# Four of twelve conditioning chunks moved from the first stage into the next one's projections

## The reference

```python
def adaln(cond, w, b):
    mod = (jax.nn.silu(cond) @ w + b).reshape(cond.shape[0], 6, D_MODEL)
    return tuple(mod[:, i][:, None, :] for i in range(6))

sh1, sc1, g1, sh2, sc2, g2 = adaln(c_ctx[None, :], ada_w[l], ada_b[l])
h = rmsnorm(xp, norm1[l]) * (1.0 + sc1) + sh1
out, k_c, v_c, s_f, s_b = token_mixer(h, w_in[l], ...)
xp = xp + g1 * out
h = rmsnorm(xp, norm2[l]) * (1.0 + sc2) + sh2
xp = xp + g2 * conv_ffn(h, w_up[l], conv_w[l], conv_b[l], w_down[l])
```

## Time and profile before

| | us |
|---|---|
| median of 3 runs | 2784.21 |
| lowest and highest | 2783.48, 2798.66 |
| the profiled execution's own time | 2790.27 |
| its span | 2788.5 |
| TensorE, weight loads | 2653.8, 2430.7 busy |
| VectorE, ScalarE, GpSimd | 1664.8, 1026.6, 808.1 busy |

### The profile page before, as it was taken

One profiled execution on the slowest core, in us unless ns is written; L12 is line 12 of the kernel. 1 busy time (PEld: TensorE's weight loads), 2 busy tenths in 40 slices (PEclk: granted clock), 3 DMA queues, 4 the chain that ended last, 5 costly groups with the idle time before them and its releaser, 6 DMA issues. The chain is left out here.

```text
span 2788.5 us, 41208 instructions
## 1 busy us (share of the span) xinstructions
PE 2653.8 (95%) x15025; PEld 2430.7 (87%) x15025; DVE 1664.8 (60%) x2673; ACT 1026.6 (37%) x1899; POOL 808.1 (29%) x775
## 2 busy tenths in 40 slices
PE   5899999999999799999999989799999999999998
PEld 2799999999999787768878867599999999999997
DVE  3245355355455447776777666635677766677765
ACT  3223233223223126666666656533221222221214
POOL 0222122122122143252253231743323232323232
PEclk8999999999999799999999989899999999999999
DMA  9311111111111110020020010331111111111101
GB/s 372 118 38 44 34 39 42 34 40 40 34 41 32 45 34 8 1 60 2 7 68 8 1 51 1 99 98 31 53 45 38 45 38 45 38 45 38 45 23 75
DMA packets 164251, 135.99 MB, mean 49 GB/s; under 512 B 18460, under 2 KB 141884, under 8 KB 164156
## 3 DMA queue, kind: packets, MB, share of 16 engines
q1 hardware_dynamic: 162940, 130.02, 14.8%
q10 hardware_dynamic: 1216, 4.72, 0.4%
HBM read 120.44 MB, written 14.29 MB: 48 GB/s over the span
## 5 line engine op out<-in xcount | busy, mean ns | idle before, releaser
L335 PE MATMUL proj_ps<-act_hi,w_hi 128*128 128x384 f32 x1152 | 410.9, 357 | 6.5 <-POOLq L473 6.5
L335 PE MATMUL ffn_ps<-act_hi,w_hi 128*128 128x384 f32 (+2 forms) x1128 | 385.1, 341 | 12.9 <-PEq L976 8.1
L336 PE MATMUL proj_ps<-act_lo,w_hi 128*128 128x384 f32 x1152 | 390.7, 339 | 0.0
L337 PE MATMUL proj_ps<-act_hi,w_lo 128*128 128x384 f32 x1152 | 390.5, 339 | 0.0
L336 PE MATMUL ffn_ps<-act_lo,w_hi 128*128 128x384 f32 (+2 forms) x1128 | 383.9, 340 | 0.0
L337 PE MATMUL ffn_ps<-act_hi,w_lo 128*128 128x384 f32 (+2 forms) x1128 | 383.9, 340 | 0.0
L2394 DVE SCALAR_TENSOR_TENSOR resid_t<-ffn_ps,mod,resid_t 128x384 f32<-128x384 f32 (+2 forms) x640 | 273.9, 508 | 140.8 <-PE ffn_ps L337 140.8
L1747 DVE TENSOR_TENSOR probs_lo<-att_ps,probs_hi 128x512 fp32r<-128x512 f32 x324 | 223.1, 689 | 157.0 <-ACT att_ps L1544 153.2
L1543 ACT ACTIVATE probs_hi<-att_ps 128x512 fp32r<-128x512 f32 x324 | 193.9, 599 | 199.0 <-PE att_ps L1363 198.1
L2372 DVE SCALAR_TENSOR_TENSOR conv<-up,conv_t,conv 128x127 f32<-128x127 f32 (+1 forms) x168 | 211.9, 1320 | 77.8 <-ACT conv L2300 66.0
L483 POOL CAST w_hi<-w_raw 128x1024 fp32r<-128x1024 f32 x48 | 61.8, 1287 | 628.4 <-PE proj_ps L337 593.5
(11 more groups left out here) (286 smaller groups left out, 5860.5 us busy)
## 6 DMA issues: line engine op xcount, KB each, us to landing
w_raw<-in_w_in SPq DMA_DIRECT2D x64, 512.0 KB, 3.9
ada_w<-in_ada_w SPq DMA_DIRECT2D x12, 2048.0 KB, 14.2
w_raw<-in_w_up SPq DMA_DIRECT2D x44, 512.0 KB, 3.9
w_raw<-in_w_down SPq DMA_DIRECT2D x22, 512.0 KB, 3.6
rec_scratch<-rec_out SPq DMA_DIRECT2D x8, 576.0 KB, 2.8
out<-xy SPq DMA_DIRECT2D x9, 512.0 KB, 2.6
w_raw<-in_w_o SPq DMA_DIRECT2D x8, 512.0 KB, 5.0
xy<-in_x_sample SPq DMA_DIRECT2D x8, 512.0 KB, 5.8
```

Of the source, the lines that this page charges most:

```text
L335: nc.tensor.matmul(out, w_hi, x_hi, start=(k == 0), stop=False)
L336: nc.tensor.matmul(out, w_hi, x_lo, start=False, stop=False)
L337: return nc.tensor.matmul(out, w_lo, x_hi, start=False, stop=last)
```

## The change

Phase 0 handles only eight chunks, in the order 0, 2, 1, 3, 4, 5, 6, 7. The first two give the shift and scale of x's first four column blocks, and the next two those of the other four, so x's parts 0 to 11 need only two chunks. `X_FOR` is a new table: parts 0 to 3 ahead of the third chunk's columns, 4 and 5 ahead of the fourth's, then five parts each ahead of the fifth to seventh and three ahead of the eighth. The first two blocks of `w_in` are issued behind the fourth chunk, the third again at the end. Of each column block's three parts ScalarE now scales the third (`scaled_part`) as well as rounding all three, and `HF` has three buffers.

Chunks 8 to 11 (sc2 and g2) go into phase 1. They use one slot, which lies over `k_dec` and `q_dec` (now one tile). SyncE issues them among the loads of `w_in`. TensorE runs chunk i's columns behind unit i of head 0 (i from 0 to 3) and its rows behind the first group of the next unit. The stationary operand there is `C2`, two columns wide, and the PSUM bank is set to zero first. ScalarE copies out between its unit copies. VectorE adds the result to the bias kept in MOD[32:48] and makes A2 inside `gates(0)`.

```diff
-        NCOL = 12
+MOD_NOW, MOD_LATER = (0, 2, 1, 3, 4, 5, 6, 7), (8, 9, 10, 11)
+        NCOL = len(MOD_NOW)
-        HF = sb("h_f32", [P, 2, 512])
+        HF = sb("h_f32", [P, 3, 512])
-        X_FOR = {c: range(3 * (c - EARLY), 3 * (c - EARLY) + 3) for c in range(EARLY, NCOL)}
+        X_FOR = {2: range(0, 4), 3: range(4, 6), 4: range(6, 11), 5: range(11, 16), 6: range(16, 21), 7: range(21, NX)}
 # SyncE, phase 0
-                    sp.dma_start(AW[:, c % AHEAD], ada[c]).then_inc(ada_in[c % AHEAD], 16)
-                    if c == 9:
+                    sp.dma_start(AW[:, c % AHEAD], ada[MOD_NOW[c]]).then_inc(ada_in[c % AHEAD], 16)
+                    if c == 3:
                         for u in range(2):
                             sp.dma_start(WR[:, u], w_in[first_units[u]]).then_inc(w_raw_in[u], 16)
 # ScalarE, phase 0
+                def scaled_part(n):
+                    j, (t0, t1, grp) = n // 3, GR[n % 3]
+                    act.wait_ge(xt_done, n + 1)
+                    act.wait_ge(mod_ok, 3 if j < 4 else 6)
+                    if n >= 3:
+                        act.wait_ge(lo_done, n - 1)
+                    nc.scalar.activation(HF[:, n % 3, 0:(t1 - t0) * P], xps[:, n % 4, 0:(t1 - t0) * P], ACT.Identity,
+                                         scale=A1[:, j, grp:grp + 1], bias=MOD[:, j, grp:grp + 1]).then_inc(hf_done_a, 1)
+                def column_parts(j):
+                    high_part(3 * j)
+                    scaled_part(3 * j + 2)
+                    high_part(3 * j + 1)
+                    high_part(3 * j + 2)
+                parts_done = 0
                 for c in range(NCOL):
+                    while c in X_FOR and 3 * parts_done + 2 <= X_FOR[c][-1] - 3:
+                        column_parts(parts_done)
+                        parts_done += 1
                     act.wait_ge(ada_done, c + 1)
...
+                for j in range(parts_done, KC):
+                    column_parts(j)
 # TensorE, phase 0
+                columns(0)
+                columns(1)
+                rows(0)
+                rows(1)
                 pe.wait_ge(xn_done, NT)
+                for c in range(2, NCOL):
                     for n in X_FOR[c]:
                         x_part(n)
                     columns(c)
+                    if c == 3:
+                        rows(2)
+                    if c == 3 or c > 4:
+                        rows(c if c == 3 else c - 1)
                 rows(NCOL - 1)
 # VectorE, phase 0
+                nc.vector.tensor_copy(MOD[:, 32:48, :], VT[:, 32:48].unsqueeze(2).broadcast_to((P, 16, 2)))
+                nc.vector.tensor_copy(A2[:, :, :], VT[:, 56:64].unsqueeze(2).broadcast_to((P, 8, 2)))
+                nc.vector.tensor_copy(C2[:, :, :], CS[:, :, 0:2])
...
                 for n in range(NX):
+                    if n in (0, 12):
+                        first_modulation(n // 12)
+                    if n % 3 < 2:
+                        dve.wait_ge(xt_done, n + 1)
+                        if n >= 3:
+                            dve.wait_ge(lo_done, n - 1)
+                        nc.vector.tensor_scalar(HF[:, n % 3, 0:(t1 - t0) * P], xps[:, n % 4, 0:(t1 - t0) * P], ...)
                     if n:
                         low_part(n - 1)
...
 # SyncE, phase 1
+                def load_chunk(i):
+                    if i:
+                        sp.wait_ge(ada_done, i)
+                    sp.dma_start(AW, ada[MOD_LATER[i]]).then_inc(ada_in, 16)
+                load(0, 3)
+                load(0, 4)
+                load_chunk(0)
                 first_states(0)
+                load(0, 5)
+                load_chunk(1)
+                load(1, 0)
+                load_chunk(2)
+                load(1, 1)
+                load_chunk(3)
+                load(1, 2)
+                load(1, 3)
 # TensorE, phase 1
+                def chunk_columns(i):
+                    if i == 0:
+                        pe.wait_ge(ada_zero, 1)
+                    pe.wait_ge(ada_in, 16 * (i + 1))
+                    if i >= 2:
+                        pe.wait_ge(ada_out, i - 1)
+                    for k in range(KC):
+                        q = k % 4
+                        m = nc.tensor.matmul(aps[32 * q:32 * q + 2, i % 2, :], C2[:, k, :], AW[:, k, :], start=(k < 4), stop=(k >= 4))
+                    m.then_inc(ada_done, 1)
                 for u in range(NU):
+                    for g in range(NG):
+                        for part in range(3):
+                            unit_part(0, u, g, part)
+                        if g == 0 and 0 < u <= len(MOD_LATER):
+                            chunk_rows(u - 1)
+                    if u < len(MOD_LATER):
+                        chunk_columns(u)
 # ScalarE, phase 1
+                chunk_evacuate(0)
                 act.wait_ge(zero_ok, 3)
                 for d in range(2):
                     for g in range(NG):
                         evacuate(0, U_RFF + d, g, SIG[:, d], ACT.Sigmoid)
+                    chunk_evacuate(1 + d)
 # VectorE, phase 1, in gates(0) behind the wait for the first exponentials
+                    dve.wait_ge(mod_t, len(MOD_LATER))
+                    nc.vector.tensor_tensor(MOD[:, 32:48, :], MOD[:, 32:48, :], kvps[:, 0, 0:32].rearrange(...), ALU.add).then_inc(mod_sum, 1)
+                    dve.wait_ge(mod_sum, 1)
+                    nc.vector.scalar_tensor_tensor(A2[:, :, :], MOD[:, 32:40, :], 1.0, A2[:, :, :], ALU.add, ALU.mult).then_inc(mod_ok, 1)
```

More of the change, by code:

```diff
@@ L110, in build, with phase0 @@
         phase3(nc, a, sem, W, HH, HL, MOD, CW, A2, X1, w_o, w_up, w_down, ident, ones, y_prompt, y_sample)
-def phase0(nc, a, sb_, pb_, sem, W, w_in, first_units, HH, HL, ident, ones, CW, MOD, A1, A2, lb, lb1, lb1n, rgain):
+MOD_NOW, MOD_LATER = (0, 2, 1, 3, 4, 5, 6, 7), (8, 9, 10, 11)
+def phase0(nc, a, sb_, pb_, sem, W, w_in, first_units, HH, HL, ident, ones, CW, MOD, A1, A2, lb, lb1, lb1n, rgain, C2, SEL):
     with ExitStack() as ctx:
@@ L238, in rows @@
                     pe.wait_ge(ada_out, c + 1)
-                    if c >= EARLY:
+                    if c >= 4:
                         pe.wait_ge(vec_ok, 2)
                         pe.wait_ge(lo_done, 1)
-                    out = mps if c < EARLY else vps
-                    for b in range(4 * c, 4 * c + 4):
-                        m = nc.tensor.matmul(out[:, 2 * b:2 * b + 2], MR[:, c % 2, (b - 4 * c) * P:(b - 4 * c + 1) * P], SEL[:, :], start=True, stop=True)
+                    out = mps if c < 4 else vps
+                    b0 = 4 * MOD_NOW[c]
+                    for b in range(b0, b0 + 4):
+                        m = nc.tensor.matmul(out[:, 2 * b:2 * b + 2], MR[:, c % 2, (b - b0) * P:(b - b0 + 1) * P], SEL[:, :], start=True, stop=True)
                     m.then_inc(mod_t, 1)
@@ L346, in load_qkv, with phase1 @@
         sp.dma_start(WR[:, 0, :, HEAD:P], w_in64[kv + 2 * B_V]).then_inc(done, 16)
-def phase1(nc, a, sem, W, w_in64, HH, HL, ident, ones, lb, lb1, lb1n, rgain, w_in, rec_dram, out_state, spent):
+def phase1(nc, a, sem, W, w_in64, HH, HL, ident, ones, lb, lb1, lb1n, rgain, w_in, rec_dram, out_state, spent, MOD, A2, C2, SEL):
     with ExitStack() as ctx:
@@ L585, in sum_squares, with chunk_rows @@
                     nc.tensor.matmul(kvps[:, g % 2, 0:G], ones[:, :], SQ[:, g * G:(g + 1) * G], start=True, stop=True).then_inc(ss_done, 1)
-                for u in range(NU):
-                    unit(0, u)
+                def chunk_columns(i):
[8 more added lines that the diff above has]
+                    m.then_inc(ada_done, 1)
+                def chunk_rows(i):
+                    pe.wait_ge(ada_out, i + 1)
+                    for b in range(4):
+                        n = 4 * i + b
+                        m = nc.tensor.matmul(kvps[:, 0, 2 * n:2 * n + 2], MR[:, i % 2, b * P:(b + 1) * P], SEL[:, :], start=True, stop=True)
+                    m.then_inc(mod_t, 1)
+                for u in range(NU):
+                    for g in range(NG):
[5 more added lines that the diff above has]
+                        chunk_columns(u)
                 pe.wait_ge(zero_ok, 3)
+                pe.wait_ge(mod_ok, 1)
                 with pe.Fori(0, RH - 1) as r:
@@ L752, in gates @@
                         dve.wait_ge(exp_f, h * 2 + (d + 1))
+                        if behind_mod and d == 0:
+                            last_modulation()
                         last = GB[:, d, CH - 1:T:CH] if d == 0 else GB[:, d, 0:T:CH]
@@ L807, in normalise @@
                         nc.vector.tensor_tensor(OT[:, cols], OT[:, cols], RG[:, cols], ALU.mult).then_inc(rec_ready, 1)
-                gates(0)
+                gates(0, True)
                 dve.wait_ge(m_in, 16)
```

86 lines of the change are left out of this document (47 added, 39 removed).

## The result

The changed kernel takes 2757.0 us (median of 8 runs, 2754.8 to 2773.0), against 2784.0 for the kernel before on the same chip: a ratio of 0.9905, 95% interval 0.9884 to 0.9926. It gains 27 us, near 1% of the time. The prediction was 2774.6, a gain of 9.6, with a range down to 2769. The profiled execution took 2771.75 us, span 2769.9; it lies above most runs of its kernel, as the one of before does, so stages are compared by their own rows. Part of the difference is TensorE's granted clock: from 900 to 1200 us it was 0.91 in this execution, 0.94 in the one of before, and 0.96 in a second profile of the changed kernel (h1_after_again, span 2755.3).

What follows compares the result with a forecast made beforehand. The prediction took ada_w transfers plus a tail to bound the kernel up to 96.15 us, and TensorE after. Terms of -21.6 and +12.0 sum to -9.6, so 2774.6 us as median, range 2769 to 2786.

Steps and rivals of the forecast that it cites:

- any gain above 24: Whole kernel: a measured gain of more than 24 us was listed as a sign that the prediction is wrong.
- even with no cost at all in phase 1 the gain is 21.6: Whole kernel: 21.6 us as the most to gain, used to argue that no case reaches a 1% change, 27.8 us.
- the time from the first projection to the end longer by 12: From the first projection on: 12 us longer, listed as a sign that the prediction is right.
- Part 1: Phase 0: four of twelve ada_w transfers go, 21.7 us; the new chunk 7 is there at 64.1 us.
- Part 2: Phase 0, x's parts: start at 34.5 us, VectorE ends at 72.2, stage shorter by 21.6 us, bounds 17.3 and 23.4.
- the columns of chunks 4 to 7 start at 46.3, 54.0, 61.6 and 65.6: Phase 0: start times in us from laying out three engines' operations in the new order, with columns at 2.5 us.
- Rival (A): Phase 0 bound by TensorE's and ScalarE's chain at the lower clock: VectorE ends at 76.5, -17.3 us, total 2778.9; chance 0.14.
- Its tail is no shorter than before: End of phase 0: VectorE's tail stays as long, from ScalarE's last column of x and GpSimd's subtraction for the third w_in block.
- Part 3: Head 0's projections: four added chunks cost 12.0 us of TensorE, from 11.1 to 15.3; the added waits cost nothing.
- (B): Phase 1: chunk columns lose their overlap with two-column weights, 31.8 us for four chunks; total +10.2 us, 2794.4; chance 0.08.
- (C): Phase 1: chunks come late, TensorE stands some 3 us at each of three and its clock drops; +1.4, 2785.6; chance 0.06.
- (D): Phase 0: early w_in blocks leave a queue gap ahead of chunk 4, losing 5.4 of 21.6 us; 2780.0; chance 0.06.

Runs made afterwards that it cites:

- e1: The kernel before with only an unused tile of 96 bytes a partition ahead of w_raw: 2760.1 us, ratio 0.9911.
- g1: The changed kernel, but ScalarE handles a column block of x ahead of a chunk's copy whenever its transposes precede the chunk's columns: 2749.4 us, ratio 0.9872.
- e5: The kernel before with an unused tile of 32 bytes a partition ahead of act_hi, so that everything moves: 2779.4 us, ratio 0.9974.
- e6: The kernel before with an unused tile of 32 bytes a partition between act_hi and act_lo: 2777.3 us, ratio 0.9972.
- e3: The kernel before with an unused tile of 32 bytes a partition ahead of w_raw: 2758.2 us, ratio 0.9902.

## Why the prediction was wrong

The total failed for want of a term: what the moved tiles do to the products. The prediction said of the kept tiles that their copies cost "nothing", and never asked what else their 96 bytes do. They shift every tile behind them, and 22.5 us by the rows, 24.1 by e1, came of that. No rival named it, and the line "any gain above 24" among the signs of an error was the only guard. The bound for "even with no cost at all in phase 1 the gain is 21.6" was a bound on the steps considered, not on the kernel. The same shows in its sign "the time from the first projection to the end longer by 12": it is 2769.9 - 80.31 = 2689.6 us for 2788.5 - 96.15 = 2692.3, shorter by 2.7, and by 17 in h1_after_again (2755.3 - 80.09).

With placement put aside, point by point:

- Part 1, transfers: right. Four chunks are 21.7 us of transfers, and the new chunk 7 lands at 64.1, as g1 shows.
- Part 2, the parts of x: wrong by 6 us. The step that failed is the layout's "the columns of chunks 4 to 7 start at 46.3, 54.0, 61.6 and 65.6". They started 4 to 7 us later and the stage was shorter by 15.8, not 21.6. The layout chose 2.5 us for the columns, where chunks 4 and 6 took 3.58 and 3.39, and had GpSimd's holding some 2 us too late (43 to 50, in fact 41.4 to 48.1). What it had for ScalarE's order cannot be read, since its operations are not on record; g1 shows that this wait, with the clock that went along with it, was worth 8 us: there the projections start at 72.18, sooner than the 74.5 forecast. Rival (A), with chance 0.14 and -17.3 us, named the mechanism and was near its size; g1 shows the chain of engines, by taking it away, and the lower clock was seen but not tried by itself.
- "Its tail is no shorter than before": wrong, in the kernel's favour, and at odds with the layout's own 72.2 - 65.6 = 6.6. VectorE ends 77.90 - 72.50 = 5.4 us after the start of chunk 7's columns, against 93.82 - 85.89 = 7.9 before. The columns came so late that the third w_in block was on hand at 66.08 and split before the tail began, so no subtraction of GpSimd's held act_lo there. It hid part of what the circle cost.
- Part 3, the cost in phase 1: right, 12.0 forecast, 11.7 measured. The overlap with two columns of weights is the one of 32 (1.90 us for 16 instructions), so (B) is out. No wait of TensorE for a transfer after 80 us, so (C) is out. VectorE's cover is 9 us for the 8 forecast. Its sum rests on 1.92 and 1.05 us for columns and rows; they took 1.90 and 0.95.
- (D): out; chunk 7's transfer was in time.

So the staging itself gave -15.8 + 11.7 = -4.1 by the trace and -3.1 by the medians of the changed kernel and e1_pad96, where -9.6 was forecast. The sign of the staging was right and its size was not; the measured 27 us is that and 24 us of placement. The placement was luck: with `C2` and `SEL` behind the weight tiles (e2) the same change gains nothing that can be measured (ratio 1.0009).

The Trainium skill (GPSIMD Engine Reference, Key points) says that VectorE's instructions with two SBUF inputs contend with GpSimd. The trace agrees: the two-input act_lo took 1.89 us beside the subtraction, and 0.69 alone (the one of 55.92). The Trainium skill (TensorEngine Tiling (Array Packing), Key Properties) has a drain at each change of tiling mode. With 1.83 us from the start of the columns to the next product, no more is seen here than what the columns themselves take.

## What to carry to other kernels

A change that adds or removes a kept tile moves all tiles behind it; compare the addresses of the hot operands in both builds before the stages are compared, and test with an unused tile in the kernel before. In this kernel a moving tile and its weights that lie alike modulo 64 bytes save 0.08 us in each group of 24 products of 384 columns, 24 us in all, for 32 or 96 unused bytes in a partition. And when transfers leave a stage that they bounded, lay the engines' hand-written order against each other: here one condition in ScalarE's stream (work that is ready goes ahead of a copy that still waits) was worth 7.6 us, more than the whole move of the chunks.

## What the runs showed of the hardware that was not expected

- The spacing of products with 384 columns at clock 1.00 depends on how the moving operand and the weights lie to each other modulo 64 bytes: 0.173 us where both lie at 0, 0.177 where one lies at 0 and the other at 32 (act with w in before, e2 and e5; gated with w in e2). Where both lie at 32 (gated with w in before) the mean of one is 334 ns, as where both lie at 0. No other distances were tried. One tile of two out of line (e6) costs about two thirds of it in the spacing.
- Transfers of ada_w ran at 409 GB/s in the three builds whose slots begin at a multiple of 512 bytes (e3, e5, e6), and at 382 to 387 in those where they begin 64 or 480 bytes behind one (before, the changed kernel, e1, e2). This was seen only; the slots were not moved by themselves, nor was it tried with the changed order of work.
- The order with fewer gaps went along with a granted clock of 1.00 instead of 0.76 between 40 and 60 us, and gained 7.6 us where 4 were expected from the gaps alone. What of that is the clock was not tried by itself.
